# First norm of a hybrid decoder step: rows scaled and plainly transposed, instead of products with diagonal matrices

## The reference, cut to what matters

```python
def _rmsnorm(x, gain):
    xf = x.astype(jnp.float32)
    return xf * lax.rsqrt(jnp.mean(xf * xf, axis=-1, keepdims=True) + NORM_EPS) * gain

def _layer(x, ...):
    xn = _rmsnorm(x, norm1)
    proj = xn @ w_in                    # 1024 -> lru_x, lru_y, rwkv columns, two gates
    ...                                 # RG-LRU branch, RWKV-7 branch, sigmoid merge
    x = x + merged @ w_out
    x = x + _hier_moe(_rmsnorm(x, norm2), ...)   # 32 experts, two per token
    ...
```

## Time and profile before

| | |
|---|---|
| median of three runs | 781.22 us (780.98 to 782.2) |
| the profiled execution | 782.07 us |
| its span, first to last instruction | 780.3 us |
| TensorE busy | 746.7 us (96%) |
| VectorE, ScalarE busy | 441.7 us (57%), 241.0 us (31%) |
| mean granted clock of TensorE | 0.994 |
| DMA | 160.06 MB, mean 205 GB/s |

### The profile page before, as it was taken

How to read it: one execution, slowest core, us unless ns; L and a number is a source line. 1 busy time by engine, 2 the same in 40 slices (tenths; PEclk the granted TensorE clock), 3 DMA queues, 4 the chain that set the end, 5 groups by cost and what they waited for, 6 DMA issues and landing times.

```text
span 780.3 us, 18185 instructions
## 1 busy us (share of the span) xinstructions
PE 746.7 (96%) x7070; PEld 463.0 (59%) x7070; DVE 441.7 (57%) x1169; ACT 241.0 (31%) x593; POOL 61.9 (8%) x71
## 2 busy tenths in 40 slices
PE   4999999999999999999999989999899999999896
PEld 4666666666666666676666666445455555555442
DVE  3274677777777777767867864624623432322225
ACT  4234343353352451452453442222100001100014
POOL 3000000400000000000000000000123222222110
PEclk9999999999999999999999999999999999999999
DMA  9244143671160160261151461699799999999995
GB/s 250 81 112 138 29 110 98 130 186 53 27 191 13 28 193 10 65 166 27 42 163 27 149 242 35 246 400 329 296 416 417 417 419 417 421 418 420 421 407 199
DMA packets 117127, 160.06 MB, mean 205 GB/s; under 512 B 27687, under 2 KB 92001, under 8 KB 110665
## 3 DMA queue, kind: packets, MB, share of 16 engines
q1 hardware_dynamic: 100532, 147.57, 52.6%
q0 software_dynamic: 5760, 7.80, 3.9%
q10 hardware_dynamic: 10789, 4.06, 2.0%
HBM read 154.43 MB, written 15.73 MB: 218 GB/s over the span
## 4 chain that ended last, share of the span: by engine, by line
PE 89%; DMA 5%; DVE 2%; ACT 1%; issue 1%; POOL 0%; SPq 0%; POOLq 0%; ACTq 0%; DVEq 0%
PE bank L805 24%; PE bank L1218 13%; PE bank L1225 6%; PE bank L977 5%; PE bank L811 5%; PE bank L1111 4%; PE bank L1055 4%; DMA wall<-in_exp_up 3%; PE bank L777 2%; PE bank L1257 2%; PE bank L910 2%; PE bank L919 2%; PE bank L1007 1%; PE bank L839 1%; PE bank L1082 1%
## 5 line engine op out<-in xcount | busy, mean ns | idle before, releaser
L805 PE MATMUL bank<-xnT,wall 128*128 128x320 f32 x656 | 194.7, 441 | 0.0
L805 PEld LDWEIGHTS bank<-xnT,wall 128*128 128x128 f32 x656 | 118.6, 190 | 45.0 <-issue 2.6
L696 POOL DMA_INDIRECT merged<-xn2d,gidx x15 | 15.5, 1036 | 518.9 <-DVE gidx L2152 411.1
L2196 DVE COPY vecs<-bank 128x512 f32<-128x512 f32 x32 | 22.1, 691 | 57.9 <-PE bank L1225 29.4
L2201 DVE TENSOR_TENSOR scratch<-bank,n 128x512 f32<-128x512 f32 x30 | 20.5, 687 | 49.3 <-PE bank L1218 45.8
L977 PE MATMUL bank<-xnT,wall 128*128 128x320 f32 x128 | 47.9, 456 | 0.3
L1649 ACT ACTIVATE vecs<-bank 128x128 f32<-128x128 f32 x32 | 8.9, 277 | 115.7 <-PE bank L1218 115.7
L1218 PE MATMUL bank<-vecs,scratch 128*64 128x256 f32 x352 | 40.6, 382 | 0.5 <-DVE scratch L2137 0.5
L1218 PE MATMUL bank<-scratch 128*64 128x256 f32 x320 | 36.7, 382 | 3.3 <-DMA scratch<-in_exp_up 2.9
L1416 ACT ACTIVATE shared<-bank 128x256 f32<-128x256 f32 x32 | 12.3, 385 | 73.4 <-PE bank L805 66.7
L1055 PE MATMUL bank<-xnT,wall 128*128 128x320 f32 x112 | 33.1, 439 | 0.7
(11 more groups left out here) (430 smaller groups left out, 1361.9 us busy)
## 6 DMA issues: line engine op xcount, KB each, us to landing
wall<-in_w_in SPq DMA_DIRECT2D x58, 512.0 KB, 5.4
scratch<-in_exp_gate SPq DMA_DIRECT2D x10, 1024.0 KB, 14.2
scratch<-in_exp_up SPq DMA_DIRECT2D x10, 1024.0 KB, 16.6
vecs<-in_exp_gate SPq DMA_DIRECT2D x10, 1024.0 KB, 9.9
vecs<-in_exp_up SPq DMA_DIRECT2D x10, 1024.0 KB, 12.2
scratch<-in_exp_down SPq DMA_DIRECT2D x6, 1024.0 KB, 13.7
shared<-in_exp_gate SPq DMA_DIRECT2D x10, 512.0 KB, 15.0
shared<-in_exp_up SPq DMA_DIRECT2D x10, 512.0 KB, 17.2
```

Of the source, the lines that this page charges most:

```text
L805: q = mm(tpbank(L, name), wbuf[name][:, k, :], xnT[:, k, :], start=(k == 0), stop=(k == KC - 1))
L2196: CP(ye[:, e % 2, :], bank[6 + e % 2][:]).then_inc(S("ye"), 1)
```

## The change

VectorE no longer writes a diagonal matrix. It scales the rows themselves, in two halves of 512 columns, into `xn`, over the squares that nobody reads, and signals `xn` after each half. TensorE turns the scaled chunks with plain transposes (the identity as the other operand) and waits for a half instead of a tile. `rstd` goes. The gains get a semaphore (`norm1_in`), a transpose (eight rows) and a copy (eight columns) of their own, and stand first in `VEC`. The transpose of the whole block, which waits for the other twelve vectors, follows the six halves on TensorE, into bank 1; its copy of the other 120 columns follows VectorE's last `by_column`. Who reads those columns waits for `vecc` 2, and so do the state transposes, which write bank 1 next.

```diff
-VEC = {"conv_w": 0, "conv_b": 32, "lru_bx": 40, "lru_ba": 48, "a_param": 56, "w0": 64, "a0": 72,
-       "k_k": 80, "k_a": 88, "r_k": 96, "ln_w": 104, "ln_b": 112, "norm1": 120}
+VEC = {"norm1": 0, "conv_w": 8, "conv_b": 40, "lru_bx": 48, "lru_ba": 56, "a_param": 64, "w0": 72, "a0": 80,
+       "k_k": 88, "k_a": 96, "r_k": 104, "ln_w": 112, "ln_b": 120}
...
-        rstd = scratch3[:, NMU * P:NMU * P + 3 * P].rearrange("p (t c) -> p t c", t=3)
...
             pe.wait_ge(S("first_in"), 16)
-            pe.wait_ge(S("vec_in"), 16 * 7)
-            pe.wait_ge(S("pool_dma"), 16 * 6)
-            tr(bank[0][:, 0:128], vrows[:], ident).then_inc(S("vecT"), 1)
+            pe.wait_ge(S("norm1_in"), 16)
+            tr(bank[0][:, 0:KC], vrows[0:KC, :], ident[0:KC, 0:KC]).then_inc(S("vecT"), 1)
 
             for j in range(6):
...
-                pe.wait_ge(S("xn"), t + 1)
+                pe.wait_ge(S("xn"), j + 1)
...
-                    q = mm(b[:, c * P:c * P + n], xt[0:n, t, d:d + P], rstd[0:n, t, 0:n], start=True, stop=True)
+                    q = tr(b[:, c * P:c * P + n], xn[0:n, t, d:d + P], ident[0:n, 0:n])
                 q.then_inc(S("xT_ps"), 1)
+            pe.wait_ge(S("vec_in"), 16 * 6)
+            pe.wait_ge(S("pool_dma"), 16 * 6)
+            tr(bank[1][:, 0:128], vrows[:], ident).then_inc(S("vecT"), 1)
 
             def states():
 
                 pe.wait_ge(S("st_in"), 16 * 7)
+                pe.wait_ge(S("vecc"), 2)
...
-            for name, key in VECTORS[:7]:
+            act.dma_start(vec_rows("norm1"), vec_src("norm1", "norm1")).then_inc(S("norm1_in"), 16)
+            for name, key in VECTORS[1:7]:
                 act.dma_start(vec_rows(name), vec_src(name, key)).then_inc(S("vec_in"), 16)
...
-            act.wait_ge(S("vecc"), 1)
+            act.wait_ge(S("vecc"), 2)
...
                 ch.step(nc.vector.reciprocal(rowst[0:n, 6 + t:7 + t], rowst[0:n, 3 + t:4 + t]))
-                TS(rstd[0:n, t, 0:n], ident[0:n, 0:n], rowst[0:n, 6 + t:7 + t], None, MUL).then_inc(S("xn"), 1)
+                for h in range(2):
+                    c = slice(512 * h, 512 * h + 512)
+                    TS(xn[0:n, t, c], xt[0:n, t, c], rowst[0:n, 6 + t:7 + t], None, MUL).then_inc(S("xn"), 1)
...
             dve.wait_ge(S("vecT"), 1)
-            CP(vT[:], bank[0][:, 0:128]).then_inc(S("vecc"), 1)
+            CP(vT[:, 0:KC], bank[0][:, 0:KC]).then_inc(S("vecc"), 1)
             by_row(1)
             dve.wait_ge(S("vecc"), 1)
             by_column(0)
             by_row(2)
             for j in range(1, 6):
                 by_column(j)
+            dve.wait_ge(S("vecT"), 2)
+            CP(vT[:, KC:], bank[1][:, KC:128]).then_inc(S("vecc"), 1)
+            dve.wait_ge(S("vecc"), 2)
             for j, n in enumerate(("w0", "a0", "lru_bx", "lru_ba")):
...
-            dve.wait_ge(S("vecT"), 2)
+            dve.wait_ge(S("vecT"), 3)
...
```

## The result

The changed kernel takes 776.63 us (median of 4 executions, 775.43 to 778.58) against 781.1 for the kernel before on the same chip: 4.5 us less, ratio 0.9943 with a 95% interval of 0.9915 to 0.997. Forecast were 778.7 and a range from 776.9 to 781.4. The gain is larger than forecast, and it is rival 1 that came, whose price was 777.2.

A forecast was written before the change was run, and what follows sets the result against it. The prediction took TensorE, with 89% of the chain, as the bound, its first long product delayed by the opening. An earlier start of 4.0 less 1.5 for the clock gave 2.5 us: 778.7, range 776.9 to 781.4.

The forecast's parts named there:

- rival 1: In the opening, the transposes raise TensorE's clock, so the shared projections start fast: 777.2 us or a little less; chance 0.22.
- Term one: In the opening, the shared projections start at 13.8 instead of 17.83 us: 4.0 us gained.
- VectorE as the pace: In the opening, VectorE's stream ends at 13.63 us, and the projections can't start below 13.6.
- the landing of the gains: In the opening, `norm1` lands at about 5 to 7 us, which nothing waits for.
- one record per transpose: On TensorE in the opening, transposes take one record each where products took two: 24 for 48.
- the price of a scaling: On VectorE in the opening, a 128x512 scaling takes 0.488 us, two in a row starting 0.33 apart.
- One for one to the end: From the shared projections' start to the kernel's end, an earlier start than 17.83 us shifts the end equally.
- term two: In the shared projections, transposes don't raise the clock, so the first records run slow: 1.5 us lost.
- Rival 3: The clock stays low through both full-width projections, costing another 8.9 us: 786.1 us; chance 0.07.
- Rival 2: No change: in the opening `norm1` lands late, toward 10.1 us, or scalings run at 0.61: 780.4 to 781.1; chance 0.16.

The follow-up runs named there:

- early table: The changed kernel with ScalarE's first table load moved ahead of six of its DMA issues; 776.56 us, ratio 0.9942 to the kernel before.
- lead_transposes: The changed kernel with 44 unread 128x128 transposes of the identity ahead of the gains' transpose, run twice; 785.32 and 785.04 us.
- again: The changed kernel itself, unaltered, run once more beside the others on the same chip; 777.54 us, ratio 0.9947 to the kernel before.
- spread: The changed kernel with the 36 small state transposes spread between the second projection's products; 777.13 us, ratio 0.9941 to the kernel before.
- both: The changed kernel with the edits of spread and early table together; 778.53 us, ratio 0.9967 to the kernel before.
- burst: The changed kernel with all 24 transposes held until all rows are scaled, third tile scaled ahead of the first gain; 781.64 us in one execution.
- vectors alone: The kernel before with only the gains' own load and turn, products with diagonals kept; 780.46 us, ratio 0.9979 to the kernel before.
- identity products: The changed kernel with plain products with the identity in place of the 24 transposes; 780.21 us, ratio 0.9979 to the kernel before.
- warmed: The changed kernel with nine unread plain products on ones, 320 columns each, ahead of TensorE's first wait; 781.0 us in one execution.
- lead_products: The changed kernel with 22 unread plain products with the identity ahead of the gains' transpose, run twice (a, b); 783.92 and 782.04 us.
- held: The changed kernel with the shared projections held until the rest of the constants has landed; 783.6 us in one execution.
- transposes alone: The kernel before with only the scaled rows and plain transposes, all vectors still first; 779.73 us, ratio 0.9972 to the kernel before.

## Why the prediction was wrong, step by step

Term one held. Forecast 4.0 from 13.8; measured 13.55 and 13.93, gains of 4.28 and 3.90. VectorE as the pace, the landing of the gains, one record per transpose, the price of a scaling (starts 0.40 apart, not 0.33): near enough to the sum, and the two parts measured apart account for it. One price in it was wrong without harm: the last eight transposes (64 rows) were taken at 0.213 like the others, but at the lower level they come 0.10 to 0.17 apart (early table), so that TensorE is done before VectorE at either level. One for one to the end is right as far as it can be read: 4.29 at the first turn, 4.5 in the medians.

The step that failed is term two, at the words "so I take transposes as not raising the clock". The row under it, 27 transposes of 8 columns 0.065 apart, is of another kind than 24 full ones 0.21 apart, and the text said so, but still gave the case 0.55. Run alone, full-width transposes raise the clock (lead_transposes). In the changed kernel's own profile the last eight transposes come 0.06 to 0.14 apart from 11.4 us on, at the full level; early table's same eight stay 0.10 to 0.17 apart. The last nine in the changed kernel, then in early table:

```profile
11.09 1.12 PE L758 MATMUL bank<-consts_sb,scratch 128*128 128x128 f32 x9
...
11.10 1.47 PE L758 MATMUL bank<-consts_sb,scratch 128*128 128x128 f32 x9
```

That the projections find the clock up is, however, not assured by that. Of five profiles with the changed kernel's opening and nothing ahead of it or held (the changed kernel, again, spread, early table, both), four have fast projections, and one, early table, slow ones: 10.38 instead of 8.88, a loss of 1.50. That is term two's price, though not for its reason, since the same transposes had raised the clock in the changed kernel's profile. The price falls due in the lesser part of executions, as far as five profiles tell, and not in the likeliest. As an average it would be 0.3 (an estimate from these five), and 4.0 less that is 3.7; the three comparisons with the changed kernel or with early table in it stand at 4.2 to 4.7.

So the time is rival 1's, 777.2 forecast and 776.63 measured, 0.3 under the range's lower end. The rest of the difference is not settled: 0.25 of it is the earlier root in that profile, and the executions lie up to 3 us apart. Those differences go with the mean granted clock: 775.43 at 0.997, 778.58 at 0.993. Of the kernel before's 26 executions on the chip of spread and early table, the four at 0.998 or more take 778.2 to 779.3 us, the eight at 0.992 or less 781.8 to 785.4. Rival 3 (low through both projections) did not come; the longest low stretch in the projections was that of the two lead_transposes runs, 18.15 to 24.2. Rival 2's late landing is excluded by 5.16.

The sentence of the Trainium skill, "TensorE: Matmul & The Clock Gate", Part 4: PE-mode transpose, that the full level doesn't engage for transpose-mode work as it does for matmuls, disagrees with lead_transposes, where the spacing fell from 0.21 to 0.11 twice among transposes alone. The measurement decides.

Left open: why burst stayed slow for 9 us after its start, 5 of transposes and 3.8 of projections, and early table for 8.9, where the long transposes of lead_transposes needed 5.5. A third of burst's transposes have half the columns, and two starts lie 0.35 and 0.59 apart, but no run separates these. They can't be the whole of it: up to 11.1 us TensorE's records in early table lie within 0.02 us of the changed kernel's, yet the first fast record comes at 11.4 in the changed kernel and at 16.8 in early table. What TensorE did up to then does not tell the two apart.

## What to carry to other kernels

Where a first stage waits for the last of many small loads, find which of them it needs and give that one its own semaphore; the new start is read from the next engine's stream, here VectorE's, ahead of which it can't come. A row about the clock tells of the work that it shows; with a row of another kind, the case deserves a run or an even chance, not the forecast. A clock that an opening raises can still be low at the next stage, in some executions: price it as a chance, not as a term. And before an edit is credited with a clock that stayed up, look how often it stayed up without the edit: here in six of 14 profiles.

## What the runs showed of the hardware that was not expected

The moment of the rise wanders. From TensorE's first dense work to the first fast record it took 2.7 us in the kernel before, then 3.8, 4.7, 5.4, 4.4 and 5.2 where products came first (vectors alone, identity products, warmed, lead_products a and b), and 3.6, 4.2, 4.0, 3.7 and 4.2 where transposes did (the changed kernel, again, spread, held, transposes alone), 5.5 in the two lead_transposes runs. In the run both the transposes are slow to their end and the projections, 5.7 us after the start, fast; in early table and burst it took 8.9 and 9.1 us, and the first fast record is one of the projections'.

Interleaving small transposes with wide products doubles their cost: four add 0.54 to a product (1.08 against 0.54), where 27 in a row take 1.77, or 0.26 for four.
